# Two stacked transformer-like layers in split fp32: weight sums of a seven-product scheme made ahead in buffers of their own, and two convolution groups interleaved at the start

## The reference, cut to what matters

```python
def hybrid_layer(x, ...):                       # layer 1
    proj = einsum("bsd,de->bse", x, w_in) + b_in
    c_val, c_glu, c_gate, q, k, v, a_gate = split(proj)
    y_conv = conformer_conv_branch(c_val, c_glu, conv_w, ...)   # GLU, 31 taps, layer norm
    y_attn = swa_sink_attention(q, k, v, sinks) * silu(a_gate)
    return layer_norm(ALPHA * x + concat([y_conv * silu(c_gate), y_attn]) @ w_out + b_out)

def hybrid_layer_2(x, mem, ...):                # layer 2: sparse attention, gated linear attention,
    ...                                         # cross attention to mem, then
    hf = rms_norm(x, g_ffn)                     # the feed-forward part, D_FF = 5632
    gg, uu = split(hf @ w_gu)                   # w_gu: 2048 x 11264
    return x + (silu(gg) * uu) @ w_down         # w_down: 5632 x 2048
```

## Time and profile before

| | |
|---|---|
| Median of 3 runs | 1599.85 us (1598.87 to 1601.6) |
| The profiled execution | 1599.53 us |
| Its span in the trace | 1597.7 us |
| TensorE busy | 1581.3 us, 99% |
| VectorE busy | 1195.6 us, 75% |
| ScalarE busy | 816.5 us, 51% |
| Granted TensorE clock | 1.00 throughout |

### The profile page before, as it was taken

The page is one execution under the profiler, slowest core; times in us unless marked ns, Lnnn a source line. Parts: engine busy times, 40 slices in busy tenths (PEclk is TensorE's granted clock), DMA queues, the critical chain, the costliest instruction groups (busy, mean ns, idle before and its releaser), DMA issues.

```text
span 1597.7 us, 22903 instructions
## 1 busy us (share of the span) xinstructions
PE 1581.3 (99%) x8735; PEld 1341.2 (84%) x8735; DVE 1195.6 (75%) x1664; ACT 816.5 (51%) x1122; POOL 159.8 (10%) x245
## 2 busy tenths in 40 slices
PE   8999999999999999999999999999999999999999
PEld 8999889888877888788888888888888888888887
DVE  5989898789765796976666788888654678888644
ACT  4455664655544654664464755555443455555432
POOL 3000000310100141000003011110200001111100
PEclk9999999999999999999999999999999999999999
DMA  9655445698576485448554666666755467666663
GB/s 318 219 162 188 139 154 170 185 309 296 200 264 214 139 271 182 138 164 295 201 184 156 217 230 205 215 224 206 249 196 195 147 211 237 237 231 216 218 204 106
DMA packets 177418, 331.21 MB, mean 207 GB/s; under 512 B 8899, under 2 KB 45041, under 8 KB 176160
## 3 DMA queue, kind: packets, MB, share of 16 engines
q1 hardware_dynamic: 167184, 298.05, 55.8%
q0 software_dynamic: 10128, 31.72, 6.4%
HBM read 312.95 MB, written 16.78 MB: 206 GB/s over the span
## 4 chain that ended last, share of the span: by engine, by line
PE 88%; DVE 5%; issue 4%; ACT 2%; DMA 1%; POOL 1%; SPq 0%; DVEq 0%; ACTq 0%; POOLq 0%
PE ps_g L434 23%; PE ps_g L436 22%; PE ps_g L435 22%; PE ps_g L479 4%; PE ps_g L480 4%; PE ps_g L481 4%; DVE lo L512 2%; ACT hi L497 2%; PE ps_m L356 1%; DVE raw L533 1%; PE ps_g L1593 1%; DMA raw<-in_w_in_dram 1%; PE ps_g L1595 1%; PE ps_g L1594 1%; DVE guL L2980 1%
## 5 line engine op out<-in xcount | busy, mean ns | idle before, releaser
L497 ACT CAST hi<-raw 128x1024 fp32r<-128x1024 f32 (+3 forms) x581 | 590.0, 1021 | 671.9 <-PE ps_g L436 523.6
L512 DVE TENSOR_TENSOR lo<-raw,hi 128x1024 fp32r<-128x1024 f32 (+3 forms) x581 | 684.4, 1186 | 327.0 <-ACT hi L497 319.5
L434 PE MATMUL ps_g<-hi,aH 128*128 128x512 f32 (+3 forms) x1216 | 466.3, 383 | 0.0
L436 PE MATMUL ps_g<-hi,aL 128*128 128x512 f32 (+3 forms) x1216 | 457.4, 376 | 0.0
L435 PE MATMUL ps_g<-lo,aH 128*128 128x512 f32 (+3 forms) x1216 | 457.0, 376 | 0.0
L434 PEld LDWEIGHTS ps_g<-hi,aH 128*128 128x128 f32 x1216 | 228.8, 188 | 42.7 <-issue 2.9
L436 PEld LDWEIGHTS ps_g<-hi,aL 128*128 128x128 f32 x1216 | 228.5, 188 | 42.4
L435 PEld LDWEIGHTS ps_g<-lo,aH 128*128 128x128 f32 x1216 | 228.9, 188 | 39.4
L479 PE MATMUL ps_g<-aH,hi 128*128 128x256 f32 x512 | 146.8, 287 | 3.0 <-DVE lo L512 2.0
L481 PE MATMUL ps_g<-aH,lo 128*128 128x256 f32 x512 | 144.8, 283 | 0.0
L480 PE MATMUL ps_g<-aL,hi 128*128 128x256 f32 x512 | 144.8, 283 | 0.0
(11 more groups left out here) (472 smaller groups left out, 1756.1 us busy)
## 6 DMA issues: line engine op xcount, KB each, us to landing
raw<-in_w_gu_dram SPq DMA_DIRECT2D x88, 1024.0 KB, 6.1
raw<-in_w_in_dram SPq DMA_DIRECT2D x60, 1024.0 KB, 5.1
raw<-in_w_down_dram SPq DMA_DIRECT2D x44, 1024.0 KB, 5.2
raw<-in_w_out_dram SPq DMA_DIRECT2D x32, 1024.0 KB, 5.2
raw<-in_w_in_dram SPq DMA_DIRECT2D x42, 512.0 KB, 5.0
raw<-in_w_ck_dram SPq DMA_DIRECT2D x8, 1024.0 KB, 5.5
raw<-in_w_cv_dram SPq DMA_DIRECT2D x8, 1024.0 KB, 5.3
turned<-hb POOLq DMA_DIRECT2D x88, 64.0 KB, 4.7
```

The lines of the kernel that those rows point to most:

```text
L434: pe.matmul(dst, xh, wh, start=first, stop=False)
L436: last = pe.matmul(dst, xl, wh, start=False, stop=final)
L497: act.copy(step_view(hi, s), raw_view(s)).then_inc(s_hi, steps_done(s))
L512: dve.tensor_tensor(step_view(lo, s), raw_view(s), step_view(hi, s).bitcast(F32), ALU.subtract).then_inc(s_lo, steps_done(s))
```

## The change

In the feed-forward part, `weight_sums` is replaced by `weight_sum(dve, i, t)`, one call for each of the four sums, called by the new `sums_for` under steps 1, 2, 3 and 5 of the `fu` group ahead of the block (5, 4, 3 and 1 steps before b), behind the step's other DVE work. For block 1 these are steps 3, 4, 5 and 7 of the longer `fu0`; for block 6 they are steps of `fd03`, the last group of the first part's down projection. Sum 1 is written into a buffer `ws1` (in the place of `bias`, no longer used then) and sum 3 into `ws2` (in the place of `ts`); products 2 and 4 are split from these. Sums 2 and 4 stay in place in `raw`. The number and shapes of all operations stay as they are.

At the start, `cm0` and `cm1` are cut: `cm0first` (k tiles 0 to 3, steps 0, 1), `cm1first` (k tiles 0 to 3, steps 2, 3), `cm0` (k tiles 4 to 15, steps 4 to 9), `cm1` (steps 10 to 15). The `x` quarters are issued ahead of chunks 0, 2, 3 and 4 instead of 0, 1, 2 and 3. The transposes of `x` unit p stand behind step p for p = 2 to 7, the transposes of small parameters behind step 9 instead of 7, and the convolution begins behind step 10, with 5 operations for each of steps 11 to 18 and 4 from there to step 31.

```diff
+    for j in range(2):
+        group(f"cm{j}first", w_in, T * j, 512, kt=CHUNK, closes=False)
+    for j in range(2):
+        group(f"cm{j}", w_in, T * j, 512, kt=KT - CHUNK, k0=CHUNK, x0=CHUNK, opens=False)
-    for name, col, n in (("cm0", 0, 512), ("cm1", T, 512),
-                         ("q0", 3 * C, 512), ("q1", 3 * C + 512, 512), ("kv", 4 * C, 256),
+    for name, col, n in (("q0", 3 * C, 512), ("q1", 3 * C + 512, 512), ("kv", 4 * C, 256),
...
         def raw_view(s):
             c, n = chunk_of_step[s], step_cols[s]
+            if s in product_of and product_of[s][1] in (2, 4):
+                return (ws1 if product_of[s][1] == 2 else ws2)[:]
...
-        def weight_sums(dve, s):
-            g, j = product_of.get(s, (None, None))
-            if j not in (0, 2, 3):
-                return
+        def weight_sum(dve, i, t):
+            g = G[f"fs{i}"]
             b, n = g["s0"], 4 * g["n7"]
...
-            if j == 0:
+            if t == 0:
+                wait_raw(dve, g["c0"])
                 wait_raw(dve, g["c0"] + 1)
-                dve.wait_ge(s_lo, b + 1)
-                dve.tensor_tensor(b11, b12, b11, ALU.subtract).then_inc(s_sums, 1)
+                dve.tensor_tensor(ws1[:], b12, b11, ALU.subtract).then_inc(s_sums, 1)
+            if t == 1:
+                dve.tensor_tensor(b12, b22, b12, ALU.subtract).then_inc(s_sums, 1)
+            if t == 2:
                 dve.wait_ge(s_sums, n + 1)
-                dve.tensor_tensor(b12, b22, b12, ALU.subtract).then_inc(s_sums, 1)
-            if j == 2:
-                dve.wait_ge(s_lo, b + 3)
-                dve.tensor_tensor(b11, b22, b11, ALU.subtract).then_inc(s_sums, 1)
-            if j == 3:
+                dve.wait_ge(s_tsl, 1)
+                dve.tensor_tensor(ws2[:], b22, ws1[:], ALU.subtract).then_inc(s_sums, 1)
+            if t == 3:
+                dve.wait_ge(s_lo, b + 2)
                 dve.wait_ge(s_sums, n + 3)
-                dve.tensor_tensor(b21, b21, b11, ALU.subtract).then_inc(s_sums, 1)
+                dve.tensor_tensor(b21, b21, ws2[:], ALU.subtract).then_inc(s_sums, 1)
...
+        X_BEFORE = (0, 2, 3, 4)
...
-                if c < 4:
-                    sp.dma_start(x[:, :, c * NG:(c + 1) * NG],
+                if c in X_BEFORE:
+                    q = X_BEFORE.index(c)
+                    sp.dma_start(x[:, :, q * NG:(q + 1) * NG],
...
-                    if g["i"] == 0 and j < 6:
-                        x_T([j + 2])
-                    if g["i"] == 0 and j == 7:
+                    if 2 <= p < 8:
+                        x_T([p])
+                    if p == cm_end[0] - 1:
                         param_columns()
...
-                    weight_sums(dve, q)
                     split_to[0] = q + 1
 
             for u in range(8):
                 build_dve(dve, "x", A(aH), A(aL), only=[u])
-                keep_up(u - LEAD if u < 2 else u - 2)
-            keep_up(7)
+                keep_up((-LEAD, 1)[u] if u < 2 else u)
+            keep_up(cm_end[0] - 1)
...
-                if 9 <= p < kv:
-                    rate = 4
+                if cm_end[0] < p < kv:
+                    rate = 5 if p <= cm_end[0] + 8 else 4
...
+                    if i + 1 < g0 + n:
+                        sums_for(i + 1, u["s0"] + j)
+
+            def sums_for(i, p):
+                before = G[f"fs{i}"]["s0"] - p
+                if before in (5, 4, 3, 1):
+                    weight_sum(dve, i, (5, 4, 3, 1).index(before))
```

More of the change, by code:

```diff
@@ L182, in stack_kernel @@
                 chunks[-1]["halves"] = [g["w"][:, h * C:(h + 1) * C].rearrange("(k p) n -> p k n", p=P)[
-                    :, CHUNK * c:CHUNK * (c + 1), g["col"]:g["col"] + T] for h in range(2)]
+                    :, k:k + CHUNK, g["col"]:g["col"] + T] for h in range(2)]
             g.setdefault("c0", len(chunks) - 1)
@@ L460, in gemm_T @@
             s = g["s0"] + j
-            if j == 0 and g["turn"] >= 1:
+            if j == 0 and g["opens"] and g["turn"] >= 1:
                 pe.wait_ge(s_free[pair_of(g)], TT * g["turn"])
@@ L473, in gemm_T @@
                 kk = STEP * j + k
-                first, final = kk == 0, kk == g["kt"] - 1
+                first, final = g["opens"] and kk == 0, g["closes"] and kk == g["kt"] - 1
+                kk += g["x0"]
                 for ct in range(n // P):
@@ L713, in stack_kernel @@
         ts = put("ts", 200, [P, 4, STEP, P])
+        ws1 = put("ws1", small_at["bias"], [P, STEP * NG])
+        ws2 = put("ws2", 200, [P, STEP * NG])
         s_sums = sem("weight_sums_made")
@@ L837, in _ @@
                         sp.dma_start(w_c2[:, i], a[w][0].rearrange("(k p) n -> p k n", p=P)).then_inc(s_p2, 16)
-                if c < 4:
-                    sp.dma_start(x[:, :, c * NG:(c + 1) * NG],
-                                 a["x"][0].rearrange("(t p) d -> p t d", p=P)[:, :, c * NG:(c + 1) * NG]
-                                 ).then_inc(s_x[c], 16)
+                if c in X_BEFORE:
+                    q = X_BEFORE.index(c)
+                    sp.dma_start(x[:, :, q * NG:(q + 1) * NG],
+                                 a["x"][0].rearrange("(t p) d -> p t d", p=P)[:, :, q * NG:(q + 1) * NG]
+                                 ).then_inc(s_x[q], 16)
                 if g is not None and g["name"] in bias_groups and c == g["c0"]:
@@ L1007, in stack_kernel @@
         first_wo = G["wo0first"]["s0"]
+        cm_end = [G[f"cm{c}"]["s0"] + G[f"cm{c}"]["ns"] for c in range(4)]
         nsa_units = {3 * (u // 2) + u % 2 - 3: u for u in range(2 * QH)}
@@ L1126, in before_y @@
                     pe.wait_ge(s_pTc, HEADS)
-            for g in groups[:11]:
+            for g in groups[:13]:
                 for j in range(g["ns"]):
@@ L1133, in _ @@
                     else:
-                        gemm_T(pe, g, j, (lambda j: pe.wait_ge(s_xl, built("x", 2 * j + 2))) if g["i"] == 0 else None)
-                    if g["i"] == 0 and j < 6:
-                        x_T([j + 2])
-                    if g["i"] == 0 and j == 7:
+                        gemm_T(pe, g, j, (lambda j: pe.wait_ge(s_xl, built("x", g["x0"] + 2 * j + 2)))
+                               if g["name"] in ("cm0first", "cm0") else None)
+                    if 2 <= p < 8:
+                        x_T([p])
+                    if p == cm_end[0] - 1:
                         param_columns()
@@ L1164, in y_operand @@
                 return lambda k, n: first[:, k:k + n, :] if k < 8 else second[:, k - 8:k - 8 + n, :]
-            for g in groups[11:17]:
+            for g in groups[13:19]:
                 for j in range(g["ns"]):
@@ L1374, in _ @@
             lq1 = G["lq1"]["s0"]
-            for g in groups[18:31]:
+            for g in groups[20:33]:
                 for j in range(g["ns"]):
@@ L1456, in _ @@
             hq_at = {("w2o2", 1): 0, ("w2o2", 2): 1, ("w2o2", 6): 2, ("w2o2", 7): 3}
-            for g in groups[31:37]:
+            for g in groups[33:39]:
                 for j in range(g["ns"]):
@@ L1498, in pv3 @@
                 last.then_inc(s_pv3, 1)
-            for g in groups[37:39]:
+            for g in groups[39:41]:
                 for j in range(g["ns"]):
@@ L1558, in _ @@
             oc_T(1)
-            for g in groups[39:43]:
+            for g in groups[41:45]:
                 for j in range(g["ns"]):
@@ L1704, in squares @@
                     act.wait_ge(s_sqs, count + t + 1)
-            for g in groups[:17]:
+            for g in groups[:19]:
                 for j in range(g["ns"]):
@@ L1709, in _ @@
                     here = (g["name"], j)
-                    if g["i"] == 0 and j < 6:
-                        build_act(act, "x", A(aH), only=[j + 2])
-                    if g["i"] == 0 and j == 0:
+                    if 2 <= p < 8:
+                        build_act(act, "x", A(aH), only=[p])
+                    if p == 0:
                         split_hi(act, 2)
@@ L1715, in _ @@
                     for c in range(4):
-                        if p == G[f"cm{c}"]["s0"] + 8:
+                        if p == cm_end[c]:
                             conv_gate(c)
@@ L2995, in _ @@
                     g = G[f"fd{part}{i}"]
-                    keep_up(g["s0"] + g["ns"] - 1)
+                    end = g["s0"] + g["ns"]
+                    if g["name"] == "fd03":
+                        for p in range(end - 5, end - 1):
+                            keep_up(p)
+                            sums_for(PARTS[1][0], p)
+                    keep_up(end - 1)
+                    if g["name"] == "fd03":
+                        sums_for(PARTS[1][0], end - 1)
                     if g["name"] != "fd13":
```

## The result

| | before | after |
|---|---|---|
| Median of 6 runs | 1600.01 us (1597.87 to 1602.12) | 1591.02 us (1590.41 to 1592.38) |
| Profiled execution / its span | 1599.53 / 1597.7 us | 1591.21 / 1589.0 us |
| TensorE busy | 1581.3 us | 1580.1 us |

The ratio is 0.9944, 95% interval 0.9931 to 0.9957. In a second comparison on another occasion it was 0.9945 (0.9931 to 0.9959; 1590.64 us beside 1599.32). The forecast was 1591.2 us. The total was right, but its terms were off in both directions. The time outside the span grew with the change, from 1.8 to 2.2 us: it is 1.7 to 2.1 us in every run of the kernel before that lists its span, and 2.1 to 2.3 us in every run of the changed kernel.

A forecast was written before the change was run, and what follows sets the result against it. TensorE was taken as the bound, busy 1581.3 of 1597.7 us. Taking 7.7 us (blocks) and 0.9 (start) off the profiled 1599.5 gave 1590.9, plus 0.3 for the median 1591.2 us; range 1589.9 to 1595.0.

The forecast's parts named there:

- The loss in the blocks and its cause: Ten product windows lose 8.2 us: product 5's `lo` is late behind `ups`, another `lo` and sum 4 on DVE.
- the 0.5 us of block 6: Block 6 has no `ups` yet loses 0.5 us; taken as speaking against `ups` being the bound.
- The sums' part, 7.7 us: Feed-forward blocks: sums moved out of the products win 8.2 us, less 0.5 given back at b+8; bounds 3.2 and 8.2.
- The start, 0.9 us: Chunk 1 ahead of x quarter 1: 1.8 us won, less 0.84 for two transpose units; bounds -0.5 and 1.3.
- the quarter holds chunk 1 up by 1.8 us: At the start, quarter 1 lands at 11.0 behind chunk 0 at 9.2; without it ahead, chunk 1 lands at 13.0.
- The estimate of 1.2 us for the quarter: At the start, fixed latency plus 512 KB at 436 GB/s: chunk 1 held up 1.2 us, start gives 0.4 us.
- Chunk 2 and step 4: At the start, chunk 2 lands about 18.7; PE can start step 4 at 21.8, wants 22.1: room 0.3 us.
- The new wait for `raw`: Sum 1, 5 steps ahead of b, waits for both chunks; DVE waits 0.4 us in block 3, hidden under `fu`.
- rival 3: Slower: a late second chunk blocks DVE, shifting sums and all `lo`; 1610 at 4 us late; chance 0.03.
- My threshold: In block 3, DVE decides from a second-chunk landing at 1002.5, 2.1 us later; each further us costs one a block.
- The convolution at rate 5: A fifth operation for eight steps: DVE falls back up to 3.4 us plus 0.9, room 6.1 us, cost nothing.
- The rivals: Stall moves to b+8 or b+6, 0.12; start gives nothing, 0.10; DVE blocked by late chunk, 0.03; DVE bound otherwise, 0.05.

The follow-up runs named there:

- `x_order_old`: The changed kernel with the x quarters issued ahead of chunks 0, 1, 2, 3 as before, groups still interleaved; 1592.85 us, ratio 0.9961.
- `ahead7`: The changed kernel with sums 1 and 2 made 7 and 6 steps ahead of the block instead of 5 and 4; 1591.36 us, ratio 0.9953.
- `ahead8`: The changed kernel with sums 1 and 2 made 8 and 7 steps ahead of the block instead of 5 and 4; 1605.7 us, ratio 1.0042.
- `sums_only`: The kernel before with the new places and buffers of the weight sums alone; 1593.35 us, ratio 0.9963.
- `start_only`: The changed kernel with `weight_sums` as before, so the start's part alone; 1597.33 us, ratio 0.9989.

## Why the prediction was right, point by point

- **The loss in the blocks and its cause.** Right. Two edits that differ by one DVE operation of 1.1 us differ by 0.6 us a block, in the nine blocks with `ups` and not in block 6. Two readings of it were loose: ten pieces of 1.14 us or more are 11.4 us and up, not "ten to eleven", and the 0.5 us of block 6 were taken as a sign against `ups` alone without a look at the other piece in the row there.
- **The sums' part, 7.7 us.** Measured 7.4 us from the first product to the end of the last window. The excess of 8.2 us went in full, but 0.1 us a block came back at b+8 where the earlier trace rows showed 0.05; the tenth of these lies behind the last window, which leaves 7.3 us in all. In the earlier trace rows the `lo` was ready 0.17 us ahead of its matmul, and the second matmul came 0.28 us behind the first; after the change it came at 0.30, and the next two are spaced 0.24. That a split released just in time is behind it is borne out by the kernel without the null step.
- **The start, 0.9 us.** This is the term that was mis-sized: 1.8 us at step 16. The step that failed is "the quarter holds chunk 1 up by 1.8 us", read from two landings. Its own transfer took that time, but chunk 1's cast began 2.7 us earlier without it in front (14.84 to 12.17; 2.3 us between `x_order_old` and the changed kernel). So step 2 began at 14.63 and not at 15.5, and 2.66 less 0.84 us are the 1.8. The price of the two transposes, 0.84 us, fits (steps 2 to 4 after are 3.3 us apart). The estimate of 1.2 us for the quarter, worked out from the Trainium skill ("SBUF — State Buffer", The DMA setup-cost knee), was further off.
- **Chunk 2 and step 4.** No wait, as forecast. Chunk 2 came 1.4 us earlier than worked out, but PE also wanted it 0.9 us earlier, so the room was 0.9 us where 0.3 was forecast.
- **The new wait for `raw`.** Free here, as forecast; in block 3 after, the chunk was there before DVE came. `ahead7` and `ahead8` show the mechanism of rival 3: nearly harmless while inside the room (1.6 us for 34.7 us of waits), then worse than worked out. My threshold counted DVE's work alone and left out that ACT's SiLU, and the casts behind it, wait for `gate_rows`.
- **The convolution at rate 5.** No cost, and the room, 6.1 us as worked out, is about 6.2 us by the kernel that overran it.
- **The sum.** 7.7 + 0.9 = 8.6 against 7.3 + 1.8 - 0.4 = 8.7 us of span: the terms' errors, -0.4 and +0.9, and the drift of the layers between, -0.4, cancelled. Two more errors did too. The prediction kept the time outside the span at 1.8 us, and it was 2.2: this goes with the new sums (2.1 to 2.3 us in `sums_only`, 1.8 to 1.9 in `start_only`), for a reason that no run shows, and costs some 0.3 us of the gain. And the median was put 0.3 us above the profiled execution, and was 0.2 below it. That the total came within 0.2 us is luck to that extent.
- **The rivals.** None occurred: all windows 9.52 us, no wait at step 4, product 5 in time, and no block lost by a late second chunk.

What stays open: why a 512 KB quarter in front delays a later transfer by more than the quarter's own time. In the kernel before, the two halves of chunk 1 landed 1.3 and 2.5 us behind the transfer ahead of each; in the changed kernel it was 0.9 and 2.1 us. So about 0.8 of the 2.7 us lie in chunk 1's own halves, with the quarter's 1.8 beside them. The transfers overlap at the start, and no run says why these intervals differ. Open too is the longer time outside the span.

## What to carry to other kernels

When one engine makes operands for another in program order, work that fits on average can still be late where several extra pieces fall into a short stage; move the pieces to where each step has idle time, and give them their own buffers where writing in place would have to wait for the stage's own splits. Then look for the next release that is only just in time, often already visible in one odd block of the trace before. A wait put into such a queue costs little up to the room of everything behind it, on every engine that waits for that queue, and the room ends abruptly: count the other engine's queue too.

## What was not expected of the hardware

The start's transfers: chunk 1's two halves, issued at 4.7 and 5.2 us behind the 512 KB quarter and at 4.2 and 4.7 us without it, were both there for the first cast at 14.5 to 14.8 us (three profiles) and at 11.9 to 12.4 us (nine profiles): some 2.1 to 3.0 us for half a MB, while the quarter's landing came only 1.8 us behind the one ahead of it. And DVE could stand still for 34.7 us in all with only 1.6 us lost on PE in the feed-forward part, but 55.5 us cost some 14 us (1605.7 against 1591.36 us).
